# Gates of 384 tokens scattered by adding indirect DMAs instead of one-hot matmuls, with the search run block by block and the rests of the first expert table split between GpSimd and VectorE

## The reference, cut to what matters

```python
def peer_ffn(h, w_query, sub_keys, u_tab, v_tab):      # 8 heads, 128 keys twice, top 16, 16384 experts
    q = (h @ w_query).reshape(bsz, seq, PEER_HEADS, 2, PEER_HALF)
    scores = jnp.einsum('blhcd,hckd->blhck', q, sub_keys)
    s_top, i_top = lax.top_k(scores, PEER_TOPK)
    cand_s = s_top[..., 0, :, None] + s_top[..., 1, None, :]           # 16 x 16 sums
    cand_i = i_top[..., 0, :, None] * PEER_KEYS + i_top[..., 1, None, :]
    best_s, pos = lax.top_k(cand_s, PEER_TOPK)                          # (both reshaped to 256 first)
    expert_idx = jnp.take_along_axis(cand_i, pos, axis=-1)
    gates = jax.nn.softmax(best_s, axis=-1)
    ...
        act = jax.nn.gelu(jnp.einsum('td,thkd->thk', h_blk, u_tab[i_blk]))
        return jnp.einsum('thk,thkd->td', g_blk * act, v_tab[i_blk])
```

## Time and profile before

| what | value |
|---|---|
| three timed runs | 3099.11, 3129.53 and 3127.0 us; median 3127.0 |
| the profiled execution's own time | 3085.22 us |
| its span, first to last instruction | 3083.4 us |
| mean granted TensorE clock | 0.988 |
| TensorE matmul busy | 2993.4 us (97%) |
| VectorE, ScalarE, GpSimd busy | 2037.5, 1228.6 and 745.1 us |
| time of the stage of U, from the timeline | about 1733 to 2505 us |
| time of the stage of V | 2512.6 us to the end |

### The profile page before, as it was taken

How to read it: one execution, slowest core, us unless ns; L and a number is a source line. 1 busy time by engine, 2 the same in 40 slices (tenths; PEclk the granted TensorE clock), 3 DMA queues, 4 the chain that set the end, 5 groups by cost and what they waited for, 6 DMA issues and landing times.

```text
span 3083.4 us, 37566 instructions
## 1 busy us (share of the span) xinstructions
PE 2993.4 (97%) x13961; PEld 2466.0 (80%) x13961; DVE 2037.5 (66%) x3402; ACT 1228.6 (40%) x2166; POOL 745.1 (24%) x443
## 2 busy tenths in 40 slices
PE   8999999999999989999999999999999988999999
PEld 7877787877877756676677888888888878999999
DVE  6678534447798889934754589767770026878887
ACT  4266232224323332122533323399992222333332
POOL 0000000003304000000000244433334454656651
PEclk9999999999999999999999999999999998999999
DMA  6156435554354455433113244456767466999996
GB/s 219 51 194 215 143 114 204 191 174 171 122 192 156 156 209 168 145 116 123 48 55 96 88 131 143 138 169 182 219 191 222 140 227 224 346 361 349 348 368 218
DMA packets 310391, 564.92 MB, mean 183 GB/s; under 512 B 124344, under 2 KB 164408, under 8 KB 309824
## 3 DMA queue, kind: packets, MB, share of 16 engines
q1 hardware_dynamic: 185376, 460.18, 43.6%
q0 software_dynamic: 22528, 67.19, 5.7%
q10 hardware_dynamic: 102304, 35.13, 4.4%
HBM read 489.51 MB, written 139.98 MB: 204 GB/s over the span
## 4 chain that ended last, share of the span: by engine, by line
PE 88%; DVE 7%; issue 2%; ACT 2%; DMA 1%; POOL 0%; SPq 0%; ACTq 0%; DVEq 0%
PE psum L669 88%; DVE wl L1528 1%; ACT wh L1107 1%; DVE yb L1740 0%; DVE psum L1904 0%; DVE trig L1623 0%; DMA xc<-xc 0%; DVE trig L1626 0%; DVE lb L1731 0%; DVE trig L1628 0%; DVE trig L1625 0%; DVE trigw L1627 0%; DVE trigw L1624 0%; DVE st L1981 0%; DVE cs L1738 0%
## 5 line engine op out<-in xcount | busy, mean ns | idle before, releaser
L669 PE MATMUL psum<-h_hi,wh 128*128 128x512 f32 x2144 | 856.9, 400 | 31.2 <-DVE h_lo L1672 13.2
L669 PE MATMUL psum<-h_hi,wl 128*128 128x512 f32 x2144 | 849.6, 396 | 0.0
L2306 POOL TENSOR_TENSOR wl<-ring,wh 128x1024 fp32r<-128x1024 f32 x170 | 422.7, 2487 | 1766.3 <-ACT wh L1107 1766.3
L669 PE MATMUL psum<-h_lo,wh 128*128 128x512 f32 x2144 | 849.2, 396 | 0.0
L1107 ACT ACTIVATE wh<-ring 128x1024 fp32r<-128x1024 f32 (+2 forms) x492 | 504.5, 1028 | 603.6 <-PE psum L669 505.3
L1528 DVE TENSOR_TENSOR wl<-ring,wh 128x1024 fp32r<-128x1024 f32 (+2 forms) x322 | 375.8, 1171 | 519.4 <-ACT wh L1107 467.8
L669 PEld LDWEIGHTS psum<-h_hi,wh 128*128 128x128 f32 x2144 | 406.3, 190 | 133.1 <-issue 39.5
L669 PEld LDWEIGHTS psum<-h_hi,wl 128*128 128x128 f32 x2144 | 405.5, 189 | 95.5
L669 PEld LDWEIGHTS psum<-h_lo,wh 128*128 128x128 f32 x2144 | 406.2, 189 | 89.6 <-issue 1.7
L669 PE MATMUL psum<-ews_hi,wh 128*128 128x384 f32 x1024 | 349.8, 342 | 14.1 <-DVE wl L1528 8.3
L669 PE MATMUL psum<-ews_lo,wh 128*128 128x384 f32 x1024 | 349.3, 341 | 3.7 <-issue 3.7
(11 more groups left out here) (398 smaller groups left out, 4135.2 us busy)
## 6 DMA issues: line engine op xcount, KB each, us to landing
ring<-tables SPq DMA_DIRECT2D x256, 512.0 KB
rows_scratch<-tables SPq DMA_DIRECT2D x128, 512.0 KB, 5.0
acts_scratch<-ga SPq DMA_DIRECT2D x128, 256.0 KB, 2.2
gates_scratch<-stage ACTq DMA_DIRECT2D x6, 4096.0 KB, 21.5
abuf<-acts_scratch SPq DMA_DIRECT2D x128, 192.0 KB
gbuf<-gates_scratch SPq DMA_DIRECT2D x128, 192.0 KB
ring<-w_up SPq DMA_DIRECT2D x44, 512.0 KB
ring<-w_modb SPq DMA_DIRECT2D x32, 512.0 KB
```

What stands on the lines that cost most here:

```text
L669: return nc.tensor.matmul(out, lhsT, rhs, start=first, stop=last, **kw)
L2306: g.tensor_tensor(wl, slot(WHOLE_OF[e], 0, D), wh.bitcast(F32), ALU.subtract)\
```

## The change

Gates of the first three blocks are no longer built by matmuls. SP fills `gates_scratch` with zeros, in 16 DMAs of 1.57 MB from a zeroed row in SBUF, one behind the load of each query tile. VectorE makes, for each pick, the element number in `gates_scratch` (first key x 128 + second key, x 384, + token), and GpSimd issues 384 indirect DMAs that each add one column of 128 gates to 128 such elements (`spread`, now in GpSimd's program). Two follow each of `low("ui14")` to `low("ui25")`, the rest come behind. The order over blocks and heads is `HEAD_ORDER`; before a head's first scatter GpSimd waits until all earlier scatters of that block have landed.

```diff
+KEYS_PER = 4
+EXP_AT = (9, 20, 33, 47)
+UI_BY_GP = 26
+LOW_EVERY = 17
+SPREAD_FROM = 14
+HEAD_ORDER = [(0, 0), (0, 1), (0, 2), (0, 3), (0, 4), (1, 0), (0, 5), (1, 1), (0, 6), (1, 2), (0, 7), (1, 3), (2, 0),
+              (1, 4), (2, 1), (1, 5), (2, 2), (1, 6), (2, 3), (1, 7), (2, 4), (2, 5), (2, 6), (2, 7)]
+SCATTERS = [(tb, h, k) for tb, h in HEAD_ORDER for k in range(TOPK)]
+GATES_AT = 122
...
 # SP
-            stream("query", "w_query", 16)
+            sp.wait_ge(S("cum_zero"), 2)
+            for u in range(16):
+                fetch(TILE[f"query{u}"], io["w_query"][u])
+                sp.dma_start(gates_d[:, u * JG:(u + 1) * JG, :], zeros.to_broadcast([P, JG, TD]))\
+                    .then_inc(S("gates_zeroed"), 16)
...
-                if j == SPREAD_AT + TD // 4 // SPREADS + 6:
-                    for k in range(2):
-                        sp.wait_ge(S(f"gates_parked{k}"), 16 * (TD // TG // 2))
+                if j == GATES_AT:
+                    for tb in range(NB - 1):
+                        sp.wait_ge(S(f"scattered{tb}"), 16 * PK)
                     for b in range(NV):
                         gated(b)
...
 # TensorE: turn_picks and spread go, four key scores behind each of ui0 to ui2
+                if v == 1:
+                    pe.wait_ge(S("ea_ready"), PK)
...
-            pe.wait_ge(S("ea_ready"), PK)
-            pe.wait_ge(S("gates_staged"), TD // 4)
...
 # ScalarE: key_copy writes over pq, shares_of and park_gates go
-                A(scb[:, n % 4, :], bank(b), ACT.Copy).then_inc(S("sc_ready"), 1)
+                A(pq[:, n, :], bank(b), ACT.Copy).then_inc(S("sc_ready"), 1)
...
+                if j in EXP_AT:
+                    act.wait_ge(S("best_ready"), EXP_AT.index(j) + 1)
                     A(bexp, fa, ACT.Exp).then_inc(S("best_exp"), 1)
...
+                if j in (PK - 2, PK - 1):
+                    for b in range(2 * (j - PK + 2), 2 * (j - PK + 3)):
+                        high_of_gated(b)
...
 # VectorE
+            def paced(ins, work):
+                beat[0] += work
+                if beat[0] >= LOW_EVERY:
+                    beat[0] -= LOW_EVERY
+                    if ui_low[0] < PK:
+                        low(HALF[TILE[f"ui{ui_low[0]}"]])
+                        ui_low[0] += 1
+                return ins
...
+            for tb in range(NB):
+                block_picks(tb, 1 if tb >= 2 else 0)
+            while ui_low[0] < PK:
+                low(HALF[TILE[f"ui{ui_low[0]}"]])
+                ui_low[0] += 1
...
 # GpSimd
+            gp.wait_ge(S("merged2"), KD)
+            g.memset(zeros, 0.0).then_inc(S("cum_zero"), 1)
+
+            def spread(n):
+                tb, h, k = SCATTERS[n]
+                c = h * TOPK + k
+                if k == 0:
+                    if h:
+                        gp.wait_ge(S(f"scattered{tb}"), 16 * h * TOPK)
+                    else:
+                        gp.wait_ge(S("picks_ready"), tb + 1)
+                g.indirect_dma_start(out=gates_d.rearrange("p j t -> (p j t)").unsqueeze(1),
+                                     out_offset=bass.IndirectOffsetOnAxis(
+                                         ap=picks[:, tb, c:c + 1].bitcast(U32), axis=0),
+                                     in_=picks[:, tb, 2 * P + c:2 * P + c + 1], in_offset=None,
+                                     compute_op=ALU.add).then_inc(S(f"scattered{tb}"), 16)
+            done = 0
+            for j in range(UI_BY_GP):
                 low(f"ui{j}")
+                if j == SPREAD_FROM:
+                    gp.wait_ge(S("gates_zeroed"), 16 * 16)
+                if j >= SPREAD_FROM:
+                    for n in range(2):
+                        spread(done)
+                        done += 1
+            for n in range(done, len(SCATTERS)):
+                spread(n)
```

More of the change, by code:

```diff
@@ L396, in build @@
         eq, prod = (ar(n, B + 16400 + k * 2048, 1, 2048)[:, 0, :] for k, n in enumerate(("eq", "prod")))
[L397 to L402, removed]
+        zeros = ar("zeros", B + 26128, 1, TD)
         ga4 = ar("ga4", B + 24080, 4)
@@ L2140, in _, with block_picks @@
-            for tb in range(NB):
+            def block_picks(tb, work):
+                at = slice(tb * P, (tb + 1) * P)
+                for n0 in range(0, 16, 4):
+                    ve.wait_ge(S("sc_ready"), n0 + 4)
+                    top16([tops[:, tb, n * TOPK:(n + 1) * TOPK] for n in range(n0, n0 + 4)],
+                          [topi[:, tb, n * TOPK:(n + 1) * TOPK].bitcast(U32) for n in range(n0, n0 + 4)],
+                          [pq[:, n, at] for n in range(n0, n0 + 4)], P, work)
@@ L2141, in _ @@
                 v.tensor_copy(topf[:, tb, :], topi[:, tb, :].bitcast(U32)).then_inc(S("topf_ready"), 1)
[L2142 to L2143 removed]
+                ve.wait_ge(S("topf_ready"), tb + 1)
                 for h0 in range(0, PH, 4):
@@ L2147, in _ @@
                         s1 = tops[:, tb, (2 * (h0 + j) + 1) * TOPK:(2 * (h0 + j) + 2) * TOPK]
-                        TT(t3(cand[:, j, :], TOPK), s0.unsqueeze(2).to_broadcast([P, TOPK, TOPK]),
-                           s1.unsqueeze(1).to_broadcast([P, TOPK, TOPK]), ALU.add).then_inc(S("cand_ready"), 1)
+                        paced(TT(t3(cand[:, j, :], TOPK), s0.unsqueeze(2).to_broadcast([P, TOPK, TOPK]),
+                                 s1.unsqueeze(1).to_broadcast([P, TOPK, TOPK]), ALU.add).then_inc(S("cand_ready"), 1),
+                              2 * work)
                     ve.wait_ge(S("cand_ready"), PH * tb + h0 + 4)
@@ L2152, in _ @@
                     top16([best[:, r] for r in rows], [posn[:, r].bitcast(U32) for r in rows],
-                          [cand[:, j, :] for j in range(4)], TOPK * TOPK)
+                          [cand[:, j, :] for j in range(4)], TOPK * TOPK, 1.4 * work)
                 b3 = t3(best, TOPK)
@@ L2215, in _ @@
-            for n in (TD // 4 - 2, TD // 4 - 1):
-                stage_gates(n)
+                link(TT(t3(to, TOPK), t3(bexp, TOPK), grec.unsqueeze(2).to_broadcast([P, PH, TOPK]), ALU.mult))
+                first, second = picks[:, tb, 0:P], picks[:, tb, P:2 * P]
+                if tb < NB - 1:
+                    link(STT(fa, first, float(P), second, ALU.mult, ALU.add))
+                    link(TS(fb, fa, float(TD), token[:, tb:tb + 1], ALU.mult, ALU.add))
+                    v.tensor_copy(first.bitcast(U32), fb).then_inc(S("picks_ready"), 1)
+                else:
+                    link(STT(fa, second, float(P), first, ALU.mult, ALU.add))
+                    link(v.tensor_copy(row_of, fa))
+                    link(TS(fb, fa, float(T), token[:, tb:tb + 1], ALU.mult, ALU.add))
+                    v.tensor_copy(act_of, fb).then_inc(S("picks_ready"), 1)
```

179 lines of the change are left out of this document (40 added, 139 removed).

## The result

| | before | after |
|---|---|---|
| median of the timed runs | 3113.97 us (4 runs, 3099.11 to 3129.53) | 3208.91 us (4 runs, 3201.13 to 3218.86) |
| the profiled execution: time, span, clock | 3085.22, 3083.4 us, 0.988 | 3205.8, 3203.7 us, 0.963 |

The ratio is 1.0312, 95% interval 1.0271 to 1.0352: 3.1% slower, where 1.4% faster was forecast. It lies above the upper end of the range, 3172 us.

What follows compares the result with a forecast made beforehand. PE was taken to bound the kernel while U streams; 45.1 + 1.5 + 2 - 5 = 43.6 us off the earlier median of 3127.0 gives 3083.4 us, 1.4% faster; own range 3055 to 3096, whole range 3050 to 3172.

Steps and rivals of the forecast that it cites:

- the price of a scatter: On POOL, 360 scatters alone from about 1889: 1.38 us each, bounds 1.25 and 2.2, break-even 1.49, end at 2406.
- rival A: At SP's wait behind tile 122: the scatters set SP's release; 1.72 us each, 83 us late, time 3167; chance 0.20.
- A second term of the same sum: SP's queue before V: SP must be free by 2445, with some 12 us of loading and splitting ahead of 2457.
- What PE loses: PE while U streams: gate matmuls behind tiles 46 to 93 go, 45.1 us; nine transposes of picks go, 1.5 us.
- The turn: PE's 8.30 us stand between tile 127 and the second table: two roundings made a tile earlier, 2 us gained.
- Zeros: 16 writes of 1.57 MB between the loads of w_query: hidden by the ring's lead, 0; without it up to 9 us.
- DVE: VectorE's search and subtractions during U: 70 us a block against PE's 70, keeps step; cost 0, bounds 0 and 9 us.
- rival C: VectorE falls behind in blocks 2 and 3, stretched by POOL's descriptor writing: 9 us or twice that, 3101; 0.22 with rival B.
- Waits between heads: POOL waiting for an earlier head's scatters where heads of one block follow each other: seven, near 3 us each, 20 us.
- The first 24 scatters: POOL from tile 14 on: two scatters and a subtraction take 4.9 us of a tile's 5.57, so they fit.
- Instruction gaps: PE standing with no releaser, named "issue", beside indirect DMAs: 19 us or none from 384 more; 5 us taken.
- rival B: Gaps at PE scale with the number of indirect DMAs: 19 us plus some 5 of half clock, 3102; 0.22 with rival C.

Runs made afterwards that it cites:

- the small gap: Against the changed kernel: plain instead of adding scatters, GpSimd filling a 128x128 buffer and waiting behind each; 3107.51 us (8 runs), 0.9975 of the kernel before.

## Why the prediction was wrong

**The step that failed** is the price of a scatter. The forecast bounded it by 1.25 and 2.2 us and took 1.38, by the row of the gathers, "since it is nearest to that row in operand size". It is 1.86. Operand size says little here: carried on from its two sizes an adding scatter costs some 1.25 us before its first element, and a whole plain one of 128 elements 0.97. With 360 scatters the difference of 0.48 us is 173 us, and the last one came at 2587 for 2406: SP's release, forecast 39 us early, set V's start and held PE for 163.5 us. The gather was a row for the plain scatter and met it to 0.02 us (1.27 for 1.25); for the add no row stood, and the working went to the favourable end of its own bounds where the break-even lay at 1.49. Had it taken their middle, 1.7, it would have forecast rival A. Its own two values, 1.48 up to 2015 and 1.33 behind, weigh to 1.37.

The estimate by the Trainium skill (Collectives: The Full Stack, The bandwidth ceiling: the fold count and why AG ≠ RS ≠ AR; an add needs two source reads), 1.7 us, was nearer than the row. The page says this of the reduce step of a collective and its bandwidth, not of POOL's time for small scatters. As an account of the cost it does not fit: with half the elements, and so half the reads, 1.41 of 1.56 us were left.

**A second term of the same sum** was 13 to 17 us off: SP had to be free by 2445, and really by some 2430 in terms of the last scatter's start. Some 12 us were given for loading and splitting. The timelines show 1.6 us from the last scatter's end to SP's first load, 7.2 us of SP's own issuing (the gated rows stand ahead of the first tile of V), 15 us from that tile's issue to ACT, then 11 to PE. The break-even pitch was (2430 - 1889 - 20) / 360 = 1.45.

**Rival A** has the mechanism right: place, order of the release, and a stall that grows by count times pitch. At its 1.72 it gave 83 us; at 1.86 its formula gives an end at 1889 + 670 + 20 = 2579 and a stall of 134. With the end 8 us later (2586.9) and the need some 15 us earlier this is near the measured +155.

**What PE loses** was right: 45.1 and 1.5 us forecast, 44.2 measured to the end of U, which came at 2460 for 2457. **The turn** gained 3.4 us for the 2 forecast, where nothing held it (4.9 for 8.30). **Zeros:** 0, as forecast; PE's waits from 1600 to 1800 us are those of before. **DVE:** 0 was right, and rival C is refuted: PE waited 1.1 us for rests from 1800 us to the end of U, three times, for POOL's and never for VectorE's. What the forecast left out is the other direction, a scatter made longer by VectorE's rest: it cost next to nothing at a pitch of 1.86, and 0.15 us a scatter in the run with half the elements (1.86 for 1.71). **Waits between heads:** seven of some 3 us forecast, 20 us; six came, 14.5 us in all. **The first 24 scatters** were to fit beside POOL's subtractions in 4.9 us a tile. They took 6.0 (from 1821.70 to 1827.73 for two and a subtraction, which went from 2.40 to 2.98 us), more than the tile's 5.57; PE lost 1.1 us by it.

**Instruction gaps**, forecast at 5 us and in rival B at 19 by the number of indirect DMAs: both the term and the rival had the wrong quantity. 384 adding scatters brought no gap in U. Of the 9.2 us by which V grew 4.6 are of this kind (17.0 us of issue for 12.4), 3.2 are longer matmuls in V's three groups (1051.4 for 1048.2 us busy), and 1.4 stay unassigned. What the runs showed instead is the distance: a long series 1.27 us apart makes PE stand, one 1.47 us apart does not. The argument against B, that five later bursts of sixteen gathers had none, fits this if a short burst does little; how long a series must be was not measured.

**The medians.** The forecast added 41.8 us to the profiled span's result to come to the median, a difference for which it had no reason. (Its sum for the low end gives 3050, and the range stated beside it starts at 3055.) It did not carry over: the kernel after had 3.1 us between its profiled execution and its median. By profiled executions the change cost 120.6 us, by medians 94.9. In the two kernels with gaps behind every gather the four runs lie within 5.3 us, where those of the kernel before lie within 30 in its first comparison and 8 in this one. That the gaps themselves vary from run to run would explain it; of the kernel before no long run has a profile, so this stays open.

## What to carry to other kernels

An operation that no row shows, and whose break-even lies inside its own bounds, is not priced by its nearest-looking relative: give the bad side its share, or forecast by the middle. Count the instructions of an indirect DMA stream and not its elements, and look both at the end of the stream (who waits for the last one, and what is queued behind that wait) and at its pitch: in a long series 1.27 us apart TensorE stood before each matmul, and a fill of 0.22 us with a wait behind each scatter ended that. A cheaper instruction is not a gain by itself: with the plain scatter, 0.6 us cheaper, the kernel took 3457 us, with the adding one 3209. Look too at what a neighbour does at the instant an indirect DMA starts: one that fell into VectorE's subtraction stood until it was done. A saved resource can be kept in part: two thirds of the change, the part that POOL can finish in time, gains where all of it loses.

## What the runs showed of the hardware that was not expected

- A series of indirect DMAs 1.27 us apart left PE with 81.8 us of work in 400, a matmul each 2.8 us, and for 20 us more behind the last of them. Loads of instructions fell from ten to one in 300 us, but so did the matmuls, 1293 to 111; what PE waited for is not shown. At 1.36 the time named issue in the profiled run was a twelfth of that at 1.27, at 1.47 none. The loss begins soon after POOL does nothing but scatters: from 1900 to 1950 us PE had 42.1 us of 50.
- Adding makes an indirect DMA of 128 single elements 1.56 us long, for 0.97 plain; with 64 elements it is 1.41.
- An indirect DMA of POOL that starts inside one of VectorE's subtractions (1.23 us) takes longer by what is left of it, less 0.13 us: up to 1.0 us more on 0.97. Started outside of one, none was longer (144 of 144 with half the elements, 211 of 211 with the small gap).
- A 128x128 fill of 0.22 us behind each gather made a kernel with nothing else changed 0.8% faster (0.9902 to 0.9935), and the waits that its profile named only "issue" were gone with it.
